# Sums of squares of attention heads: one product instead of two for linear attention, a rounded pair for differential attention

## The reference

```python
# gla_mixer: 4 heads, 256 values each
o = o * lax.rsqrt(jnp.mean(o * o, axis=-1, keepdims=True) + EPS) * g_out
o = o.reshape(Bsz, S, H * DV).astype(h.dtype) * jax.nn.silu(r)
return o @ w_o

# hybrid_layer: 4 differential heads, 128 values each, beside 8 stick-breaking heads of 64
o_diff = diff_attention(dq[0], dq[1], dk[0], dk[1], dv, lam)
o_diff = rms_norm(o_diff, subln) * (1.0 - lam_init)
o_sb = stick_breaking_attention(sq, sk, sv)
```

## Time and profile before

| | |
|---|---|
| time of 3 runs | 2820.78 us median (2819.22 to 2820.82) |
| the profiled execution | 2820.03 us, its span 2818.3 us |
| PE busy | 2794.5 us, 99% of the span |
| DVE, ACT, POOL busy | 1328.5, 816.2, 2043.4 us (47%, 29%, 73%) |
| mean granted PE clock | 0.998 |
| DMA | 242.59 MB, mean 86 GB/s |

### The profile page before, as it was taken

The page is one execution under the profiler, slowest core; times in us unless marked ns, Lnnn a source line. Parts: engine busy times, 40 slices in busy tenths (PEclk is TensorE's granted clock), DMA queues, the critical chain, the costliest instruction groups (busy, mean ns, idle before and its releaser), DMA issues.

```text
span 2818.3 us, 39309 instructions
## 1 busy us (share of the span) xinstructions
PE 2794.5 (99%) x14380; PEld 2257.1 (80%) x14380; DVE 1328.5 (47%) x1878; ACT 816.2 (29%) x1470; POOL 2043.4 (73%) x2353
## 2 busy tenths in 40 slices
PE   9999999999999999999999999999999999999999
PEld 7888888888766888888877788888887777888887
DVE  4945666044575576604765553231074545533201
ACT  3342222024475222202435422110043444211101
POOL 7958998768655788877855587777785456877774
PEclk9999999999999999999999999999999999999999
DMA  4213223233200333332212223332332222332232
GB/s 153 77 53 105 96 96 94 96 96 120 68 2 2 98 97 97 97 97 94 86 60 68 68 91 96 97 97 97 97 97 68 66 62 82 95 96 95 96 96 96
DMA packets 66507, 242.59 MB, mean 86 GB/s; under 512 B 7504, under 2 KB 7632, under 8 KB 66384
## 3 DMA queue, kind: packets, MB, share of 16 engines
q1 hardware_dynamic: 66384, 240.95, 26.6%
HBM read 238.82 MB, written 2.10 MB: 85 GB/s over the span
## 4 chain that ended last, share of the span: by engine, by line
PE 96%; DVE 2%; ACT 1%; issue 1%; POOL 0%; DMA 0%; SPq 0%; DVEq 0%; ACTq 0%
PE bank L545 28%; PE bank L547 28%; PE bank L546 28%; PE bank L1018 1%; PE bank L942 1%; PE bank L1199 1%; PE bank L1115 1%; PE bank L1158 1%; PE bank L960 1%; PE bank L1171 1%; PE bank L1096 1%; ACT n_P L1551 1%; PE bank L599 0%; DVE ss L1805 0%; PE bank L1086 0%
## 5 line engine op out<-in xcount | busy, mean ns | idle before, releaser
L504 POOL TENSOR_TENSOR w_lo<-w_raw,w_hi 128x256 fp32r<-128x256 f32 x1780 | 1480.9, 863 | 49.6 <-ACT w_hi L1458 14.6
L545 PE MATMUL bank<-XH,w_hi 128*128 128x512 f32 x2416 | 957.0, 396 | 3.6 <-POOL w_lo L504 2.0
L547 PE MATMUL bank<-XH,w_lo 128*128 128x512 f32 x2416 | 942.5, 390 | 0.0
L546 PE MATMUL bank<-XL,w_hi 128*128 128x512 f32 x2416 | 941.8, 390 | 0.0
L501 POOL CAST w_hi<-w_raw 128x1024 fp32r<-128x1024 f32 x437 | 484.0, 1108 | 622.3 <-DMA w_raw<-weights_dram 621.4
L545 PEld LDWEIGHTS bank<-XH,w_hi 128*128 128x128 f32 x2416 | 454.4, 188 | 104.4 <-issue 9.9
L547 PEld LDWEIGHTS bank<-XH,w_lo 128*128 128x128 f32 x2416 | 454.3, 188 | 96.4
L546 PEld LDWEIGHTS bank<-XL,w_hi 128*128 128x128 f32 x2416 | 454.8, 188 | 93.8 <-issue 2.6
L1820 DVE TENSOR_TENSOR X<-X,bank 128x512 f32<-128x512 f32 x63 | 43.1, 684 | 512.5 <-PE bank L547 512.2
L547 PE MATMUL bank<-hid_h,w_lo 128*128 (+1 forms) x704 | 273.9, 389 | 0.0
L545 PE MATMUL bank<-hid_h,w_hi 128*128 (+1 forms) x704 | 273.9, 389 | 0.0
(11 more groups left out here) (368 smaller groups left out, 3303.3 us busy)
## 6 DMA issues: line engine op xcount, KB each, us to landing
w_raw<-weights_dram SPq DMA_DIRECT2D x445, 512.0 KB, 3.4
x_tok<-x_dram SPq DMA_DIRECT2D x4, 512.0 KB, 5.0
out_dram<-y_tok SPq DMA_DIRECT2D x4, 512.0 KB, 4.1
const_sb<-consts_dram SPq DMA_DIRECT2D x1, 834.0 KB, 12.0
par_sb<-params_dram SPq DMA_DIRECT2D x1, 665.0 KB, 10.5
masks_in<-masks_dram SPq DMA_DIRECT2D x1, 640.0 KB, 13.0
w_raw<-weights_dram SPq DMA_DIRECT2D x2, 256.0 KB, 6.4
y_gain<-gain_out_dram SPq DMA_DIRECT2D x1, 512.0 KB, 4.5
```

What stands on the lines that cost most here:

```text
L504: ins = nc.gpsimd.tensor_tensor(w_lo[s][:, rows, :], w_raw[s][:, rows, :], w_hi[s][:, rows, :].bitcast(F32), ALU.subtract)
L545: nc.tensor.matmul(out_ap, w_hi[slot][:, j, :], xh, start=start, stop=False)
L546: nc.tensor.matmul(out_ap, w_hi[slot][:, j, :], xl, start=False, stop=False)
L547: return nc.tensor.matmul(out_ap, w_lo[slot][:, j, :], xh, start=False, stop=stop)
```

## The change

In linear attention DVE adds the second square tile of each head onto the first, in place, and PE does one float32 matmul a head. The four additions stand on DVE behind `evac(21)` and ahead of `gated(0)`; each waits for the increment of the one before.

In the hybrid layers ACT, after the square, also copies it rounded to fp32r (`h_osq_hi`); DVE subtracts (`h_osq_lo`, in place of `h_osq`); PE does two fp32r matmuls with `negones_r`, and the sign is taken back in the scale of ACT's logarithm. The new `squares_low(h)` stands on DVE behind the weights of block 5, 9 and 13 for heads 0 to 2, and for head 3 ahead of the whole chain of stick-breaking head 0.

```diff
@@ tensor, gla, behind tile 21
                         for h in range(H4):
-                            pe.wait_ge(gs["osq"], 2 * h + 2)
-                            for j in range(2):
-                                mm = nc.tensor.matmul(bank[4 + h][:, :], ones_m, g_osq[:, 2 * h + j, :], start=j == 0, stop=j == 1)
-                            mm.then_inc(gs["on"], 1)
+                            pe.wait_ge(gs["osq"], 8 + h + 1)
+                            nc.tensor.matmul(bank[4 + h][:, :], ones_m, g_osq[:, 2 * h, :], start=True, stop=True)\
+                                .then_inc(gs["on"], 1)
@@ tensor, hybrid
                 def d_sumsq(h):
                     pe.wait_ge(hs["osq"], 4 * ly + h + 1)
+                    pe.wait_ge(hs["osql"], 4 * ly + h + 1)
                     if h:
                         pe.wait_ge(hs["ors"], 4 * ly + h)
-                    nc.tensor.matmul(bank[6][:, :], ones_m, h_osq[:, :], start=True, stop=True).then_inc(hs["on"], 1)
+                    nc.tensor.matmul(bank[6][:, :], negones_r[:, :], h_osq_hi[:, h, :], start=True, stop=False)
+                    nc.tensor.matmul(bank[6][:, :], negones_r[:, :], h_osq_lo[:, :], start=False, stop=True).then_inc(hs["on"], 1)
@@ scalar, hybrid
                 def squares_of(h):
                     act.wait_ge(hs["pv"], 4 * ly + h + 1)
-                    nc.scalar.activation(h_osq[:, :], bank[3][:, :], ACT.Square).then_inc(hs["osq"], 1)
+                    own(nc.scalar.activation(h_osq[:, :], bank[3][:, :], ACT.Square))
+                    nc.scalar.activation(h_osq_hi[:, h, :], h_osq[:, :], ACT.Copy).then_inc(hs["osq"], 1)
@@ vector, gla, behind evac(21)
+                for h in range(H4):
+                    dve.wait_ge(gs["osq"], 8 + h)
+                    V.tensor_tensor(g_osq[:, 2 * h, :], g_osq[:, 2 * h, :], g_osq[:, 2 * h + 1, :], ALU.add).then_inc(gs["osq"], 1)
                 for f in range(5):
                     gated(f)
@@ vector, hybrid
+                def squares_low(h):
+                    dve.wait_ge(hs["osq"], 4 * ly + h + 1)
+                    V.tensor_tensor(h_osq_lo[:, :], h_osq[:, :], h_osq_hi[:, h, :].bitcast(F32), ALU.subtract).then_inc(hs["osql"], 1)
...
                     combine(n)
+                    if n >= 5 and (n - 5) % TT == 0:
+                        squares_low((n - 5) // TT)
                     if n in FILL:
                         evac(FILL[n])
...
                 k0 = SB_HEADS * ly
+                squares_low(DIFF_HEADS - 1)
                 for h in range(SB_HEADS):
                     dve.wait_ge(hs["ln"], k0 + h + 1)
```

More of the change, by code:

```diff
@@ L355, in build @@
         h_osq = at("h_osq", [P, T], F32, o_sq)
+        h_osq_hi = at("h_osq_hi", [P, 4, T], F32R, o_A + 16384)
+        h_osq_lo = at("h_osq_lo", [P, T], F32R, o_sq)
         h_ors = at("h_ors", [P, T], F32, o_sq + T)
@@ L418, in build @@
             "evac", "rot", "rope", "vT", "vc", "gate", "lp", "lsum", "le", "lam", "s", "mx", "exp", "w", "t", "tc", "pv",
-            "sqs", "skd", "osq", "on", "ors", "od", "odh", "odl", "z", "ln", "soft", "sphi", "sp", "cum", "a", "spv", "osc", "osh", "osl", "mevac", "mt", "m", "mh",
+            "sqs", "skd", "osq", "osql", "on", "ors", "od", "odh", "odl", "z", "ln", "soft", "sphi", "sp", "cum", "a", "spv", "osc", "osh", "osl", "mevac", "mt", "m", "mh",
             "ml")}
@@ L1749, in d_norm @@
                     act.wait_ge(hs["od"], 4 * ly + h)
-                own(nc.scalar.activation(h_ors[:, :], bank[6][:, :], ACT.Ln, bias=eps_col, scale=1.0 / (2 * DH)))
+                own(nc.scalar.activation(h_ors[:, :], bank[6][:, :], ACT.Ln, bias=eps_col, scale=-1.0 / (2 * DH)))
                 nc.scalar.activation(h_ors[:, :], h_ors[:, :], ACT.Exp, scale=-0.5).then_inc(hs["ors"], 1)
```

## The result

The changed kernel takes 2828.5 us (median of 7 runs, 2824.47 to 2830.3), the kernel before, beside it, 2820.78 (7 runs, 2815.95 to 2824.03). The ratio is 1.003, its 95% interval 1.0022 to 1.0039: slower by some 8 us. The forecast was 2825.3, a change too small for a measurement to tell from none. The time lies inside the 80% range (2819.5 to 2829), but above the forecast case's own range (2823 to 2827.5), and the loss is clear of the noise.

A forecast was written before the change was run, and what follows sets the result against it. PE was taken to bound the kernel (96% of the chain). Linear attention -1.89, early heads -2.42, last heads +5.8 and clock +3.0 sum to +4.5 us, giving 2825.3 us as the runs' median; 80% range 2819.5 to 2829.

The forecast's parts named there:

- the forecast case: Whole kernel: stalls at both last heads and two clock falls, 2823 to 2827.5 us, chance 0.53.
- Last head: Each hybrid layer: the subtraction ahead of DVE's chain to `sp(0)` delays it, so PE waits 3 to 4 us.
- +2.9: Net loss in us per hybrid layer at the last head, collisions included and clock excluded; range +2.0 to +4.7.
- Collisions were taken as 0.9 us: Last head's DVE chain beside POOL: at most five collisions, 0 to 2.7 us more, of which 0.9 was taken.
- The wait ahead of `s_scores(1)`, 0.52: Behind the last head: PE's old 0.52 us wait for DVE work disappears, a gain within the layer's sum.
- Heads 0 to 2: Six hybrid-layer places: two fp32r products replace 0.858 us, -0.404 each without a PE wait, -2.42 together.
- Linear attention: Sum of squares: four float32 matmuls fewer, -3.43 us, less a new wait of 1.54, net -1.89.
- So I cost it at nothing; if the cover of 1 us is gone, up to 1 us of the gain goes back: Linear attention, `gla_o`: DVE's queue is 2.03 us late, but idle time ahead of `evac(22)` and `evac(24)` swallows most.
- a sign of being wrong: Linear attention: DVE's lateness making PE wait in `gla_o` would show the prediction wrong.
- The clock: Behind each last head's stall of near 4 us the granted clock falls: 1.5 us each, +3.0 together (0 to 6).
- stalls: Last heads of both hybrid layers: PE's waits for DVE's delayed chain, +5.8 us for both.
- The rival of full collision: Last heads, both layers: all five POOL collisions, 4.7 us a layer, 4 in clock; +9, 2830, chance 0.14.

The follow-up runs named there:

- the filled wait: The changed kernel plus 14 unread matmuls on PE between the last head's `d_sumsq` and the cumulative sums: 2824.08 us, ratio 1.0016 to the kernel before.
- the wait alone: The kernel before plus one DVE wait for the last head's squares ahead of stick-breaking head 0's chain, no new work: 2825.5 us, ratio 1.0021.
- the moved subtraction: The changed kernel with the last head's subtraction moved to just ahead of the chain's last split `h_sp_lo`: 2818.55 us, ratio 0.9997 to the kernel before.

## Why the prediction was wrong in the direction and near in the mechanism

**Last head: right.** I had L2396 at 1.3 behind ACT's square; it is 1489.71 - 1488.41 = 1.30. From the square to the end of `h_sp_lo` I had 9.6 (1489.72 to 1499.3); it is 1498.15 - 1488.41 = 9.74. "+2.9" a layer stands against 3.0 in the kernel with the filled wait. Collisions were taken as 0.9 us; two came, 1.05 together. The wait ahead of `s_scores(1)`, 0.52, vanished as forecast. That the place on DVE and not the work makes it was shown by the wait alone (+7 by the medians, +6 by the ratio) and by the moved subtraction (no loss).

**Heads 0 to 2: right.** At the first head ACT's square takes 0.61 and the copy 0.63; the subtraction takes 0.69 at all eight. There it ends at 1415.04, and the pair's weights load at 1415.34. From the pair to the block behind it PE takes 0.57 (1415.56 to 1416.13), before it was 0.95: 0.38 a place where I had 0.404, and 0.38 or 0.39 at the other five, -2.3 for six.

**Linear attention: the step that failed is "So I cost it at nothing; if the cover of 1 us is gone, up to 1 us of the gain goes back".** The sum of squares went as worked out: wait 1.47 (forecast 1.54), gain 1.88 (1.89). Then all of it was given back, 1.89, more than the bound, and PE waited in `gla_o`, which I had named as a sign of being wrong. I had carried the lateness through on DVE alone and with the durations of before. Neither holds: instructions took longer beside GpSimd, and the chain also passes through ACT. DVE and ACT in the changed kernel, to be read beside the earlier trace rows, and behind them GpSimd in the same stretch:

```profile
179.79 5.63 DVE L2052 SCALAR_TENSOR_TENSOR g_o<-g_o,par_sb,g_r 128x512 f32<-128x512 f32 x5
...
186.60 1.24 ACT L1418 ACTIVATE g_oh<-g_o 128x512 fp32r<-128x512 f32 x2 [2.82 <-DVE g_o L2058]
...
191.63 1.16 ACT L1418 ACTIVATE g_oh<-g_o 128x512 fp32r<-128x512 f32 x2
192.30 1.92 DVE L2062 TENSOR_TENSOR g_ol<-g_o,g_oh 128x512 fp32r<-128x512 f32 x2 [1.52 <-ACT g_oh L1418]
...
201.36 0.68 DVE L1914 TENSOR_TENSOR g_r<-bank,rstd 128x512 f32<-128x512 f32 x1
...
206.56 1.12 DVE L2062 TENSOR_TENSOR g_ol<-g_o,g_oh 128x512 fp32r<-128x512 f32 x1 [0.70 <-ACT g_oh L1418]
...
180.06 1.38 POOL L503 CAST w_hi<-w_raw 128x1024 fp32r<-128x1024 f32 x1 [5.02 <-DMA w_raw<-weights_dram]
181.51 4.51 POOL L506 TENSOR_TENSOR w_lo<-w_raw,w_hi 128x256 fp32r<-128x256 f32 x4
```

The same copies of ACT and the same two `low` before:

```profile
191.53 1.15 ACT L1415 ACTIVATE g_oh<-g_o 128x512 fp32r<-128x512 f32 x2
192.20 1.30 DVE L2058 TENSOR_TENSOR g_ol<-g_o,g_oh 128x512 fp32r<-128x512 f32 x2
```

GpSimd's cast starts at 180.06, and the gates, pushed back by the additions, now run beside it and its splits to the end. The first five span 179.79 to 185.42, 5.63, where before they took 4.18; over the stretch 170 to 210 the eight gates mean 1179 ns instead of 942. That GpSimd is what stretches them is read from the two running at the same time; no run took it away.

How late DVE is shows against the rows of before, moved by the 1.92 us that this execution is ahead. At `evac(22)` it is only 0.6 late (189.50 against 188.89). But ACT's first copies `g_oh` had waited for the late gates; its next two roots and a table load stand behind them, so its third copy starts 2.0 late (191.63 against 189.61), and DVE idles 1.52 for it ahead of `low(2)`. From there to `evac(23)` four instructions are longer by 1.4 together, and that one is 3.5 late (197.86 against 194.40). `evac(24)` had 1.80 of idle time ahead of it, now has none, and starts at 201.36, while by my working, moved by 1.92, it should have been 201.1 - 1.92 = 199.2. From there to the last `low` it is another 0.7 longer. So the last input of `gla_o` came at 207.68 instead of 206.7 - 1.92 = 204.8, and PE, which wanted it at 206.04, waited 1.70.

The additions cost time three times: their own 2.8 us, the shift of the gates into GpSimd's stretch, and through the gates ACT's late copies. The wait of 1.7 is the same in all four kernels that hold this part as changed. Moved ahead of `evac(21)`, the additions leave 1.16; there the five gates take 4.18 again and `low(2)` is not late at all (190.74 against 192.20 - 1.47, the lead of that execution), so their place did make both.

**The clock: right that it falls at both, too small in size.** I took 1.5 a place, 3.0; it was 1.57 and 2.86, 4.4. The excess is all in the second layer, where the clock fell while PE still waited and stayed down for 6 us and more; I had taken the one length that the trace of before showed, 3.4 us.

**The sum.** Forecast +4.5: linear attention -1.89, early heads -2.42, stalls +5.8, clock +3.0. Measured in the trace: 0, -2.3, +6.0, +4.4, which is +8.1, and the medians differ by 7.7. Of the missing 3.6 us, 1.9 are the step in linear attention and 1.4 the clock. The forecast of +4.5 is 0.16%, which the bound of 0.2% made "no change"; +8.1 is 0.29%. The rival of full collision gave nearly the right number (2830) for a reason that did not occur: two collisions a layer came, not five.

The Trainium skill, "GPSIMD Engine Reference", section 1 on specifications, names as exposed to GpSimd the DVE instructions with two SBUF inputs or a two-port mode. By it the price would have gone toward the upper half of "+2.0 to +4.7"; I stayed at 2.9, and it came to 3.0. The trace agrees on who is exempt: L2428 (1.61 for three) and L2364 (0.68), which read PSUM, were not stretched beside GpSimd. It does not agree that to be exposed is to pay: L2433, two SBUF inputs, took 0.44 in the middle of GpSimd's splits, and the next one of its form 0.95. L2396 and L2453, both with two SBUF inputs, had begun before a cast and kept their time beside it (0.69 and 1.49); the casts took 1.34 and 1.52 instead of the 1.04 of the cast at 1416.70.

## What to carry to other kernels

Where a chain on one engine ends 0.05 us before another engine wants it, an instruction put ahead of it that waits for something later holds up the whole chain, however short it is itself: put it behind everything that does not need its result. An idle time downstream covers lateness only with durations that hold there; before it is counted, see which engine will now run beside the moved work, and follow the chain through every engine that it passes, here ACT. And a stall of about 4 us on TensorE cost more than half as much again by the clock (4.4 beside 7.7 us of waiting), so that term belongs in the sum, with a range as wide as a factor of two.

## What was not expected of the hardware

- Matmuls without use pay during a wait: the filled kernel was 3.9 us faster by ratio than the same one with PE idle for 3.87 us twice; with PE idle for 0.61 instead, the granted clock stayed at 1.00.
- Equal waits have unequal clocks behind them: 1.57 and 2.86 us lost after 3.87 each. A wait of 1.87 to 1.88 near 860 us was followed by a fall in the changed kernel and by none in the one before; the wait of 2.0 near 646 us by a fall in both the earlier trace rows.
- Where an instruction on DVE was lengthened beside GpSimd's splits, it was by about 0.5 us, whatever its size: 0.44 to 0.95 for 128x256, 0.21 to 0.75 for 128x128, 1.48 to 2.02 for 128x1280. One that began during a cast was longer by 0.8: a gate 0.75 to 1.53 (at 180.45 in the changed kernel), the cast `h_later_hi` on DVE 0.49 to 1.29 (L2436 at 1491.38 in the kernel before). So the "at most five collisions: 0 to 2.7 us" of the prediction priced the one with the cast too low.
- Two fp32r products of 512 columns with the same stationary matrix start 0.25 us apart (1415.56, 1415.81) and the next work 0.32 later, not 0.227 each.
